# A fused transformer and state-space kernel: attention-input reload, a gather's queue, the GELU's place and the row factors are rearranged

## The reference, cut to what matters

```python
# first block, layer 0 and layer 1
y = attention(h, ...)                       # ends in  o @ w_out   (steps "wout0", "wout1")
x = layer_norm(DN_ALPHA * x + gate * y)
# second block
y = s5_mixer(h_ctx, h_lat, ...)             # scan over 32 chunks forward and backward
z = gelu(y); a, g = split(z @ w_glu, 2)     # steps "value" and "gate"
y_lat = a * sigmoid(g)
x = x + gt1 * rmsnorm(y_lat, post)
h = rmsnorm(x, mlp_pre) * (1 + sc2) + sh2
x = x + gt2 * rmsnorm(square(relu(h @ w1)) @ w2, mlp_post)   # steps "in" and "out"
```

## Time and profile before

| | |
|---|---|
| median of 3 runs | 2784.24 us (2783.17 to 2787.64) |
| the profiled execution's own time | 2775.4 us |
| its span, first to last instruction | 2773.7 us |
| PE busy | 2485.1 us, 90% |
| DVE busy | 1716.3 us, 62% |
| ACT busy | 1037.8 us, 37% |
| mean granted TensorE clock | 0.924 of full |
| HBM read | 646.77 MB, 254 GB/s over the span |

### The profile page before, as it was taken

How to read it: one execution, slowest core, us unless ns; L and a number is a source line. 1 busy time by engine, 2 the same in 40 slices (tenths; PEclk the granted TensorE clock), 3 DMA queues, 4 the chain that set the end, 5 groups by cost and what they waited for, 6 DMA issues and landing times.

```text
span 2773.7 us, 42638 instructions
## 1 busy us (share of the span) xinstructions
PE 2485.1 (90%) x18079; PEld 2048.5 (74%) x18079; DVE 1716.3 (62%) x2624; ACT 1037.8 (37%) x1542; POOL 182.5 (7%) x297
## 2 busy tenths in 40 slices
PE   5799999788779799999988958699799999999996
PEld 1588887566557688789845847478599898998985
DVE  4657788688656855356534746576755477654554
ACT  0253343344352334334323312344444444343442
POOL 1112333011100000101000000000000000000000
PEclk7799999899899899989988965899899999999998
DMA  9969999686767689959776568778645588755552
GB/s 353 338 225 357 337 349 312 237 306 252 292 252 270 243 282 325 349 203 316 239 244 226 197 181 279 271 244 270 214 137 183 192 273 278 241 185 187 187 189 76
DMA packets 316573, 699.74 MB, mean 252 GB/s; under 512 B 13568, under 2 KB 14048, under 8 KB 311136
## 3 DMA queue, kind: packets, MB, share of 16 engines
q1 hardware_dynamic: 296992, 625.17, 65.0%
q0 software_dynamic: 19120, 69.75, 7.6%
q10 hardware_dynamic: 272, 2.10, 0.2%
HBM read 646.77 MB, written 56.49 MB: 254 GB/s over the span
## 4 chain that ended last, share of the span: by engine, by line
PE 73%; DVE 15%; DMA 8%; ACT 2%; issue 2%; SPq 0%; DVEq 0%; POOL 0%; ACTq 0%
PE bank L2077 71%; DVE arena L1311 5%; DMA ring<-in_a_w_in 3%; DMA ring<-in_w_mod 3%; DVE ring_lo L1311 2%; DVE sm L1311 2%; DVE arena L1319 1%; PE bank L2080 1%; DMA m_state<-MSB 1%; PE bank L2291 1%; DMA ring<-in_a_w_out 1%; DMA arena<-arena 0%; DVE LT L1319 0%; ACT att_w_hi L946 0%; DVE y_mlp L1319 0%
## 5 line engine op out<-in xcount | busy, mean ns | idle before, releaser
L1311 DVE TENSOR_TENSOR ring_lo<-ring,w_hi 128x1024 fp32r<-128x1024 f32 (+1 forms) x384 | 432.0, 1134 | 362.2 <-ACT w_hi L946 338.2
L946 ACT CAST w_hi<-ring 128x1024 fp32r<-128x1024 f32 x320 | 334.1, 1048 | 471.8 <-PE bank L2077 469.7
L1311 DVE TENSOR_TENSOR ring_lo<-ring,att_w_hi 128x1024 fp32r<-128x1024 f32 x192 | 231.9, 1222 | 230.4 <-ACT att_w_hi L946 220.9
L946 ACT CAST att_w_hi<-ring 128x1024 fp32r<-128x1024 f32 x192 | 198.6, 1048 | 357.4 <-PE bank L2077 177.5
L2077 PE MATMUL bank<-in_hi,w_hi 128*128 128x256 f32 x1024 | 289.5, 283 | 1.2 <-DVE n L1316 1.2
L2077 PE MATMUL bank<-in_lo,w_hi 128*128 128x256 f32 x1024 | 289.5, 283 | 0.0
L2077 PE MATMUL bank<-in_hi,ring_lo 128*128 128x256 f32 x1024 | 289.1, 282 | 0.0
L2077 PE MATMUL bank<-w_hi,hid_lo 128*128 128x512 f32 x640 | 257.0, 402 | 3.5 <-DVE ring_lo L1311 3.5
L2077 PE MATMUL bank<-att_w_hi,att_hi 128*128 128x512 f32 x512 | 206.3, 403 | 12.8 <-DVE ring_lo L1311 12.8
L2077 PE MATMUL bank<-ring,cpad 128*32 128x512 f32 x1408 | 195.2, 690 | 23.7 <-DMA ring<-in_w_mod 20.0
L2077 PE MATMUL bank<-ring_lo,att_hi 128*128 128x512 f32 x512 | 202.9, 396 | 0.0
(11 more groups left out here) (257 smaller groups left out, 5036.6 us busy)
## 6 DMA issues: line engine op xcount, KB each, us to landing
ring<-in_w_mod SPq DMA_DIRECT2D x192, 1024.0 KB, 9.4
ring<-in_a_w_in SPq DMA_DIRECT2D x64, 1024.0 KB, 10.3
ring<-in_w_mlp_in SPq DMA_DIRECT2D x64, 1024.0 KB, 5.2
ring<-in_w_mlp_out SPq DMA_DIRECT2D x64, 1024.0 KB, 5.1
ring<-in_kv_w_mod SPq DMA_DIRECT2D x32, 1024.0 KB, 10.6
ring<-in_b_w_in SPq DMA_DIRECT2D x32, 1024.0 KB, 7.1
ring<-in_kv_w SPq DMA_DIRECT2D x32, 1024.0 KB, 6.0
ring<-in_s_w_glu SPq DMA_DIRECT2D x32, 1024.0 KB, 5.5
```

The costliest lines, as they stand in the source:

```text
L946: a.copy(whi(h), raw_half(h)).then_inc(*o.up("whi"))
L1311: return v.tensor_tensor(dst, x, y, op).then_inc(*(to or o.up("dve")))
```

## The change

- The wait for the reloaded `x` and for the gate row moves from ahead of the steps into `finish` of the first `wout` panel, in both layers.
- SP waits for all `m_state` stores before it issues the loads of the attention stage's mods.
- The eight copies into `HC` are issued by SP, after its waits for other stores, and no longer by POOL.
- The order of channels in `zT` is changed so that its quarters 0 and 1 come from f = 0 alone. Their GELU stands behind the `z` copies of f = 0, with its scratch in `Y`; the first four weight halves of the GLU go to another buffer (`DL`) and are split ahead of the `z` copies of f = 1. The chunks of GLU weights are loaded in the matching order.
- The multiplication of `aN` and `yN` by the row is done panel by panel (`by_row`), and `bcast` stands behind steps 24 and 58. The squares of `yN` are taken panel by panel. `add_scaled` does factor and addition in one instruction for each half row.
- The second norm's factor is put on a diagonal matrix, and PE turns `xv` by a product with it (`turn_scaled`) in place of DVE's multiplication and a transpose. The fourth weight half of the first MLP step and the last mod piece stand behind the additions.
- The output goes out in four stores of 512 KB.

```diff
+ROW_AT = {N_GLU: "mix", NS - 6: "mlp"}
...
+    return reg(4096 + 1024 * q, 1024), reg((12288 if q < 2 else 8192) + 1024 * q, 1024)
...
+    t0 = 8 * (k // 4) + 4 * g2 + k // 2 % 2
     return zT.rearrange("p k (c q) -> p k q c", q=8)[:, t0:t0 + 3:2, 4 * (k % 2):4 * (k % 2) + 4, :].rearrange("p v q c -> p q v c")
...
 junk_mix, junk_mlp = reg(22528, 2048), N1[:, 2048:4096]
...
+    return at[:, 1024 * (h % 4):1024 * (h % 4) + 1024].rearrange("p (k n) -> p k n", k=2)
...
+        if key[0] == "step" and N_GLU <= key[1] < N_MLP:
+            q = (0, 2, 1, 3)[q]
...
+    sp.wait_ge(S["ms0"], 16 * 16)
+    sp.wait_ge(S["ms1"], 16 * 16)
...
+    for t2 in range(2):
+        sp.wait_ge(S["ln"], 3 + t2)
+        for a_ in range(4):
+            p0 = 32 * a_ + 16 * t2
+            sp.dma_start(HC[p0:p0 + 16], xv[:, t2, 512 * a_:512 * a_ + 512]).then_inc(S["hc"], 16)
...
+    for i, (t2, cs) in enumerate(row_halves):
+        sp.wait_ge(S["xres"], 5 + i)
+        sp.dma_start(out_v[:, t2, cs], xv[:, t2, cs]).then_inc(S["out"], 16)
+    sp.wait_ge(S["out"], 16 * 4)
...
     norm_rows(1)
-    for t2 in range(2):
-        g.wait_ge(S["ln"], 3 + t2)
-        for a_ in range(4):
-            p0 = 32 * a_ + 16 * t2
-            g.dma_start(HC[p0:p0 + 16], xv[:, t2, 512 * a_:512 * a_ + 512]).then_inc(S["hc"], 16)
...
+                if n == N_MLP - 1:
+                    continue
...
+    def mlp_squares(p):
+        for j in range(2):
+            a.wait_ge(*emptied("step", NS - 4 + p, j))
+            own()
+            act(junk_mlp[:, 0:512], yN[:, j, 512 * p:512 * p + 512], ACT.Square, *o.up("ysq"),
+                accum_out=ssq_g[:, 4 * j + p:4 * j + p + 1])
...
+        elif kind == "out" and gr == 3 and p:
+            mlp_squares(p - 1)
...
+    for q in range(2):
+        gelu_square(q)
+    for q in range(2):
+        gelu_sigmoid(q)
+    for q in range(2):
+        gelu_hi(q)
     for i in range(0, 4, 2):
         y_step(1, i)
+    a.wait_ge(S["step"], 62)
+    for h in range(8 * N_GLU, 8 * N_GLU + 4):
+        w_hi(h)
     for k in range(5, 8, 2):
         z_step(k)
+    a.wait_ge(*emptied("z", 4))
+    a.wait_ge(*emptied("z", 6))
+    for q in range(2, 4):
+        gelu_square(q)
+    for q in range(2, 4):
+        gelu_sigmoid(q)
+        gelu_hi(q)
...
+    w_hi(8 * N_MLP + 3)
+    for i, (t2, cs) in enumerate(row_halves):
+        a.wait_ge(S["xres"], i + 1)
+        own()
+        act(junk_mix[:, cs], xv[:, t2, cs], ACT.Square, *o.up("xsq"), accum_out=ssq_x[:, i:i + 1])
+        if i == 2:
+            rsqrt(st[:, 12:13], st[:, 2:3], st[:, 4:5], 6)
+    rsqrt(st[:, 13:14], st[:, 3:4], st[:, 5:6], 7)
+    a.wait_ge(S["xn"], 2)
...
+    mlp_squares(3)
+    rsqrt(st[:, 0:2], st[:, 2:4], st[:, 4:6], 8)
...
+            if h == 8 * n + 8 and N_GLU + 2 < n < N_MLP and n % 2:
+                by_row(aN, (n - N_GLU) // 2 - 1, row_mix, "gsq", "mix")
             if h == 8 * n + 11:
                 finish(n)
+                if n == N_MLP - 1:
+                    continue
...
+    def by_row(dst, p, row, squared, spread_, js=range(2)):
+        cs = slice(512 * p, 512 * p + 512)
+        v.wait_ge(*emptied("bc", spread_, 3))
+        for j in js:
+            v.wait_ge(S[squared], 2 * p + j + 1)
+            tt(dst[:, j, cs], dst[:, j, cs], row[:, cs], MUL)
...
         if kind in ("wout0", "wout1"):
+            if p == 0:
+                v.wait_ge(*emptied("bc", "m0g" if n == 0 else "m1g", 3))
+                v.wait_ge(S["x1" if n == 0 else "x_back"], 16)
...
+            if gr == 3 and p:
+                by_row(yN, p - 1, row_mlp, "ysq", "mlp")
...
-    v.wait_ge(S["x1"], 16)
-    v.wait_ge(*emptied("bc", "m0g", 3))
...
+    for q in range(2):
+        gelu_cube(q)
+    for q in range(2):
+        gelu_gate(q)
     for i in range(1, 4, 2):
         v.wait_ge(*filled("y", 1, i))
         copy(y_place(1, i), y_bank(1, i), *empty("y", 1, i))
+        if i == 1:
+            for q in range(2):
+                in_lo(HLk, HHk, zT, q, N_GLU)
+            for h in range(8 * N_GLU, 8 * N_GLU + 4):
+                w_lo(h)
     for k in range(4, 8, 2):
         v.wait_ge(*filled("z", k))
         for g2 in range(2):
             copy(z_place(k, g2), z_bank(k, g2), *(empty("z", k) if g2 else o.up("dve")))
...
+    for q in range(2, 4):
+        gelu_cube(q)
+    for q in range(2, 4):
+        gelu_gate(q)
+        in_lo(HLk, HHk, zT, q, N_GLU)
...
-    def add_gated(src, tmp_, t2):
-        for hf in range(2):
-            cs = slice(1024 * hf, 1024 * hf + 1024)
-            stt(tmp_[:, t2, cs], src[:, t2, cs], st[:, t2:t2 + 1], row[:, cs], MUL, MUL)
-        own()
-        for hf in range(2):
-            cs = slice(1024 * hf, 1024 * hf + 1024)
-            tt(xv[:, t2, cs], xv[:, t2, cs], tmp_[:, t2, cs], ADD, *o.up("xres" if hf else "dve"))
...
-        ts(yN[:, t2, :], xv[:, t2, :], st[:, t2:t2 + 1], None, MUL, None, *o.up("xn" if t2 else "dve"))
+    def row_factors(dst, row, squared, spread_, r):
+        by_row(dst, 3, row, squared, spread_, (0,))
+        v.wait_ge(S[squared], 8)
+        v.reduce_sum(st[:, 2:4], ssq_g.rearrange("p (t n) -> p t n", t=2), AX).then_inc(*o.up("dve"))
+        own()
+        ts(st[:, 2:4], st[:, 2:4], 1.0 / D, 1e-6, MUL, ADD, *o.up("var"))
+        by_row(dst, 3, row, squared, spread_, (1,))
+        newton(st[:, 0:2], st[:, 2:4], st[:, 4:6], r)
+        own()
+    def add_scaled(src, i):
+        t2, cs = row_halves[i]
+        stt(xv[:, t2, cs], src[:, t2, cs], st[:, t2:t2 + 1], xv[:, t2, cs], MUL, ADD, *o.up("xres"))
+    def x_factor(t2):
+        newton(st[:, 12 + t2:13 + t2], st[:, 2 + t2:3 + t2], st[:, 4 + t2:5 + t2], 6 + t2)
+        own()
+        ts(diag[t2], ident[:, :], st[:, 12 + t2:13 + t2], None, MUL, None, *o.up("xn"))
+    def x_var(t2):
+        v.wait_ge(S["xsq"], 2 * t2 + 2)
+        ts(st[:, 2 + t2:3 + t2], ssq_x[:, 2 * t2:2 * t2 + 1], ssq_x[:, 2 * t2 + 1:2 * t2 + 2], 1.0 / D, ADD, MUL)
+        own()
+        ts(st[:, 2 + t2:3 + t2], st[:, 2 + t2:3 + t2], 1e-6, None, ADD, None, *o.up("var"))
+    row_factors(aN, row_mix, "gsq", "mix", 5)
+    for i in range(4):
+        add_scaled(aN, i)
+    x_var(0)
+    w_lo(8 * N_MLP + 3)
+    mod_piece(N_MLP - 1, 7)
+    x_factor(0)
     mod_bias("m2d")
     own()
     stt(pcol, M("m2", 64), 1.0, C("mpre"), ADD, MUL, *o.up("scol"))
+    x_var(1)
+    x_factor(1)
     split_in("mlp", raw, pcol, M("m2", 48), HHk, HLk, N_MLP)
...
+    row_factors(yN, row_mlp, "ysq", "mlp", 8)
+    for i in range(4):
+        add_scaled(yN, i)
...
+    def turn_scaled():
+        for k2 in range(8):
+            key = ("xt", "mlp", k2)
+            room(*key)
+            for t2 in range(2):
+                if k2 == 0:
+                    p.wait_ge(S["xn"], t2 + 1)
+                for j in range(2):
+                    k = 2 * k2 + j
+                    t = mm(bank(*key)[:, 256 * j + 128 * t2:256 * j + 128 * t2 + 128], xv[:, t2, 128 * k:128 * k + 128],
+                           diag[t2], True, True)
+            t.then_inc(*fill(*key))
```

More of the change, by code:

```diff
@@ L238, in tables @@
         step(n)
-        if n in (N_GLU + 2, NS - 3):
+        if n in ROW_AT:
             for q in range(4):
-                bank.use(("bc", "mlp" if n == NS - 3 else "mix", q), GC)
+                bank.use(("bc", ROW_AT[n], q), GC)
         if n == N_MLP - 1:
@@ L560, in build @@
         ones = st[:, 126:127]
-        ssq_g = st[:, 128:136]
+        ssq_g, ssq_x = st[:, 128:136], st[:, 8:12]
+        diag = [sm[:, 1024 + 128 * t2:1152 + 128 * t2] for t2 in range(2)]
         pcol, pcol2 = st[:, 64:80], st[:, 80:96]
@@ L564, in build @@
         junk_mix, junk_mlp = reg(22528, 2048), N1[:, 2048:4096]
+        row_halves = [(t2, slice(1024 * hf, 1024 * hf + 1024)) for t2 in range(2) for hf in range(2)]
         def quarter(a, q):
@@ L1298, in scalar_program @@
                 round_of(n)
-                if n == NS - 3:
+                if n in ROW_AT:
                     bcast("mlp", row_mlp)
-            for t2 in range(2):
-                a.wait_ge(*emptied("step", NS - 1, 1))
-                own()
-                act(junk_mlp, yN[:, t2, :], ACT.Square, *o.up("xsq"), accum_out=st[:, 2 + t2:3 + t2])
-                rsqrt(st[:, t2:t2 + 1], st[:, 2 + t2:3 + t2], st[:, 4 + t2:5 + t2], 8 + t2)
+            mlp_squares(3)
+            rsqrt(st[:, 0:2], st[:, 2:4], st[:, 4:6], 8)
         def vector_program(v):
@@ L2044, in vector_program @@
-            v.wait_ge(*emptied("bc", "mix", 3))
-            row = row_mix
-            own()
-            add_gated(aN, yN, 0)
-            add_gated(aN, yN, 1)
-            for t2 in range(2):
-                v.wait_ge(S["xsq"], t2 + 1)
-                ts(st[:, 2 + t2:3 + t2], st[:, 2 + t2:3 + t2], 1.0 / D, 1e-6, MUL, ADD, *o.up("var"))
-                newton(st[:, t2:t2 + 1], st[:, 2 + t2:3 + t2], st[:, 4 + t2:5 + t2], 6 + t2)
-                own()
```

(2 more changed lines are left out.)

93 lines of the change are left out of this document (26 added, 67 removed).

## The result

The changed kernel takes 2747.06 us (median of 4 runs, 2738.57 to 2757.50); beside them the kernel before took 2783.7 us. The ratio is 0.987, with a 95% interval of 0.983 to 0.991. Forecast were 2748.9 us, a ratio of 0.9873. In two later comparisons the same changed kernel had 2737.44 us (ratio 0.9856, 0.983 to 0.9881) and 2742.9 us (0.9871, 0.9848 to 0.9894). Every ratio here is to the kernel before, measured beside that run.

A forecast was written before the change was run, and what follows sets the result against it. PE, busy 90% of the span, bounds the kernel, so time is won only where PE stands still or at the end. Terms sum to 35.3 us, taking 2784.24 to 2748.9 us; own range 2743 to 2756, with neighbours 2740 to 2760.

The forecast's parts named there:

- item 2: SP's wait for the m_state stores before the mod loads: last store lands 1.5 to 2 us sooner, gain 0.5 us.
- item 4: Start of the GLU: with GELU quarters 0 and 1 done early, PE's 14.29 us wait nearly vanishes, gain 15.1 us.
- Item 1: First wout step: the wait for the reloaded x no longer delays DVE's low half, PE resumes sooner, gain 9.1 us.
- Item 5: Way from GLU to MLP: second diagonal ready 5.2 us sooner, 1.5 us lost behind it on PE, gain 3.7 us.
- Item 8: Tail after the last product: work by panel, additions in one instruction, a smaller last store, gain 7.8 us.
- Item 3: Copies into HC issued by SP: the time is in the transfer, not the issue, gain 0.8 us.
- fast gather: Rival on the HC copies: from SP they reach 388 GB/s, gain 10 us in place of 0.8, total 2740; chance 0.07.
- slow one: Rival on the HC copies: SP's queue serves them one by one, eight need 74 us, total 2803; chance 0.03.
- rival of costly products: Rival: PE's products take 0.48 each, so GLU-to-MLP and bcast changes give nothing or less, total 2754; chance 0.07.
- Item 6: The bcast behind step 58: PE's third quarter waits for ACT's first copy, loss 1.7 us.
- Item 7: Added by_row and squares in the GLU and MLP steps: DVE and ACT have room for them, cost 0.
- failing cover of item 4: Rival at the GLU start: weights land late, DVE's low halves hold up PE's turns, half the gain lost, 2757; chance 0.12.

The follow-up runs named there:

- again: A further execution of the changed kernel with no edit, to recheck the chunk stage of layer 1: 2737.44 us, ratio 0.9856 to the kernel before.
- third: One more execution of the changed kernel with no edit: 2742.9 us, ratio 0.9871 to the kernel before.
- after: The first profiled execution of the changed kernel, the slowest of its four: own time 2757.5 us, where the median was 2747.06 us.
- the two that put all together: Changed kernel without SP's store wait, mlp row behind step 60, fifth half in GELU's gap, HC copies early on two queues, paired two ways: 2738.17 and 2737.22 us.

## Why the prediction was right, and where it was not

**What bounds it, and the sum.** PE's idle times, read from the chain and the timelines, were the right place to look: four of the six places gave what their stalls promised (the copies into `HC` gave nothing, and the store cost time), and the touched stretches give 33.9 and 34.3 us in the two profiles with the chunk stage undisturbed, for 35.3. The first median's 36.6 us hit the forecast more closely than the sum deserves, and that is luck: errors of 3 us (item 2) and 2 us (item 4) lie under it, partly offset by 1 to 1.6 us each from items 1, 5 and 8, and the two later comparisons gave 42.8 and 38.8 us. Their medians, 2737.4 and 2742.9 us, lie below the forecast's own range of 2743 to 2756.

**Item 1, right, and the bounds were good.** The stall ended at the time forecast. The gains of 6.6, 10.4 and 9.9 us lie within 6.2 to 11. That the slot loads behind it "move with PE" was right; that they might land later than PE needs them was left out, and costs 0.4 to 0.5 us in again and third and 3.0 in after, beyond the 0.36 us that before lost at the same place. The upper bound, for a clock that stays up, came true in part: over the ten microseconds behind the stall the granted clock is 0.82 in before and 0.83 in after and third, but 1.00 in again.

**Item 2 is the step that failed.** The prediction gave it a gain of 0.5 us, which it works out from no row. It said that the store would land 1.5 to 2 us sooner without the mod loads, and that the first product would end where it did. The store took 11.23 us in after and 11.41 in again, and 11.02 with the mod loads back beside it. So the mod loads are not what makes it slow. Other traffic may be: of the 32 stores of this loop in before the median landed after 4.2 us and eleven after 2.9 or less, and the last one lands at about the time at which the second of two reloads of the projections does, which SP issues 2 to 3 us ahead of it (11.01 us behind the store's issue in before, 11.73 in after). No run moved the reloads, so this is not shown. And the "2 us of DMA time" that the prediction called "really lost" stood in front of PE at once, as waits of 0.87 and 1.63 us, because PE wanted the third chunk at 758. The sign was wrong: 2.5 to 2.9 us lost for 0.5 us gained, at the lower bound of -3.

**Item 3, right in kind.** The price is in the transfer. 0.1 us in place of 0.8; the fast gather and the slow one both fell. The trap that the prediction cites from the Trainium skill (SBUF — State Buffer, SBUF: two separate sides) speaks of DVE's operations in a 2-port mode, not of all of DVE's work; with 110 GB/s from either queue, no such effect shows here.

**Item 4, right to 0.7 us at both places where PE starts.** The terms that the prediction lists from 1788.9 on add up to 1797.3 for the resumption, not to 1797.8; the measured 1797.1 lies near either. Behind the resumption 1.5 to 1.7 us are lost again to the lower clock in again and third: "the clock falls alike" was true in after (175.9 us from there, 175.7 before) and not there (177.4 and 177.1).

**Item 5, mis-sized by 1 us.** The second diagonal is there 16.5 us behind the last GLU product, where 17.7 were forecast. The four additions end 0.5 us sooner than forecast, and the factors, diagonals and bias behind the low half and the mod piece take 4.2 us, not 5.1. PE's way from there took 11.6 to 12.6 us in the three profiles of the changed kernel, for 11.9. So the rival of costly products is out. The Trainium skill (TensorE: Matmul & The Clock Gate, Terms), whose factor of four would make it 15.4 us at full clock, is not borne out: the 64 instructions of the 32 products end 11.5 us behind the second diagonal in after, the first four of them ahead of it, with waits of 3.1 us among them and at a granted clock of 0.73. The 33.6 us that the prediction gives for the way from the last GLU product in before are 33.4.

**Item 6, right.** A wait of 1.71 us for 1.7. The stretch lost 1.2 and 0.3 us in again and third, and 3.9 in after, whose first 6 us behind the first MLP product ran at 0.50 where again and third had 1.00.

**Item 7, right as far as it was tried.** The MLP's part is free, as its undoing shows. The GLU's part was not undone by itself; 175.9 us from the resumption to the last GLU product in after, for 175.7 in before, leave little room for it.

**Item 8, mis-sized by 1 us.** The three row products were done 1.73 us behind the last add, not 2.18; from the reduction to the factor, with the half row product in between, took 1.65 us for 1.98; and the four additions 4.87 for 5.04.

**Rivals.** The failing cover of item 4 was seen only in small. In three of the edited kernels (the half in the GELU's gap and the two that put all together) the second GLU chunk lands 22.8 to 23.2 us behind the first `y` product, for 21.8 in again; DVE's low halves end later, its `y` copy stands right behind them, and PE waits 1.35 to 1.49 us before its turns in place of 0.86 (in third 22.4 and 1.16). That is half a microsecond, not 8.

## What to carry to other kernels

Moving a wait to the first instruction that really needs the data is worth the whole stall, less what the queues behind now lack in head start: look up when the next load was needed, as well as when it was issued. A wait put in to "clear the way" for a transfer should be tried against the transfer's own time with and without company; here it was the same 11 us, and the wait was all cost. When one profile and the medians disagree by half the effect, cut both spans at the same instructions: stretches that no edit touches show what is only the clock.

## What the runs showed of the hardware

- A stage that no kernel changed took 116.3 us or 120 to 129 us, at a granted clock of 0.84 or 0.72 to 0.80. PE stands idle 18 times there in before, for 0.2 to 2.6 us, and one execution has 2.4 GHz where the next has 1.2. One profile is then no measure of 10 us.
- 256 KB transfers to 16 partitions each moved 110 GB/s from POOL's queue and from SP's. Two at once to partitions 0..15 and 64..79 were 2.35 us faster over eight copies (27.45 to 25.10); two at once to 0..15 and 32..47 not at all (27.47). The Trainium skill (SBUF — State Buffer, Door 1: The DMA port swizzle) gives the first pair disjoint ports and the second pair the same four, and the runs agree. The same page ("Can I just issue two DMAs to hit both halves?") says that two concurrent transfers, at partitions 0 and 64, serialize and gain only 6%; here 2.35 us are 12% of the copies' own 19.2 us, and with one queue 1.25 us ahead the copies did serialize.
- A stall of PE does not always cost the same. Ahead of the fifth half of the first GLU step a stall of 3.2 to 3.4 us was followed by ten microseconds at a granted clock of 0.70 to 0.85 in all eleven profiles that have it; in the three with a wait of 1.3 us, ahead of the sixth half, the clock stayed at 1.00. Putting the second in place of the first gave 3.9 us against again and 1.8 against after. In the first `wout` step the same stall of 2.88 us was followed by 1.00 in nine of twelve profiles and by 0.83 in three.
- Stores of 512 KB from one loop landed 2.8 to 11.3 us after their issue in before (median 4.2). For the last of them, mod loads issued beside it (11.0 to 11.7 us over four profiles) or held back (10.5 to 11.4 us over ten) made little difference.
